# Value blocks and gates of the second projection computed as rows past stationary tokens

## Chip, cores and metric

One core of a Trainium2 chip runs the whole computation in one launch. The metric is device microseconds from start to end. Three runs of the kernel before took 848.38, 850.11 and 849.87 us (median 849.87).

## The reference, cut to what matters

256 tokens of width 1024 pass two transformer blocks in float32. The second block begins with a norm and one wide projection, and the change is in that projection and in what reads it:

```python
proj = h @ w_in[l]                      # 1024 -> qa 512, ka 128, va 128, qb 512, kc 128, vc 128,
                                        #   ksl 128, vsl 128, kw 128, vw 128, gates 24, g_a 1024, g_b 1024
y_a = swa_sink_attention(heads(qa, 8), heads(ka, 2), heads(va, 2), sinks, table_a)
k_cmp = compress(heads(kc, 2), ...); v_cmp = compress(heads(vc, 2), ...)
nsa_gates = jax.nn.sigmoid(g_nsa)       # the 24 gate columns: 8 heads x 3 branches
y_b = nsa_attention(heads(qb, 8), k_cmp, v_cmp, heads(ksl, 2), heads(vsl, 2),
                    heads(kw, 2), heads(vw, 2), nsa_gates, table_b)
merged = jax.nn.sigmoid(g_a) * (y_a @ w_up_a[l]) + jax.nn.sigmoid(g_b) * (y_b @ w_up_b[l])
```

y_b is the gated sum of three attentions: over compressed blocks, over selected blocks (keys ksl, values vsl) and over a window (kw, vw). With 256 tokens the selection takes every block, so both of the latter are plain causal attention.

## The kernel before

**Units.** Every weight matrix is read in units of 1 MB (128 partitions x 2048 numbers), one after the other: SyncE's queue loads a unit into one of three slots of `raw` (`unit`, L357), ScalarE rounds it to `w_hi` (`hi`, L469 and, in loops, L476), VectorE writes the remainder `w_lo` (`lo`, L983; GpSimd helps at some stage borders), TensorE multiplies. The activations are split in the same way into `xh` and `xl`, and each product is three passes: high x high, high x low, low x high. Counting semaphores carry the order: `raw_in`, `hi_done`, `lo_done`, `unit_done`. A load of unit u waits until the low part of unit u - 3 is made.

**The second projection** is 20 units (numbers m below, U_IN2 + m in the code). A unit has 256 columns of weights. The weights stand in the array and the 256 tokens are moved past them, so that results come out with the columns on partitions and tokens along the row (`col_tile`: two halves of 24 products of 256 columns through `passes`, L1719). Units 0 to 2 have a wide form: high part against `xh` and `xl` in one product of 512 columns (`split_high`, L1750), then the low passes (`split_low`, L1758). m = 0 is key and value of the first attention (M_KA), 1 and 2 its queries, 3 the blocks to be compressed, 4 and 5 the queries of y_b, 6 key and value of the selection (M_KS), 7 those of the window (M_KW), 8, 10, 12, 14 and 16 to 19 the wide gates g_a and g_b, 9, 11, 13, 15 the compressing weights (CW). `proj_2` on VectorE drains each unit from PSUM and multiplies by the token's root (`rstd_b`); the semaphore `proj2` counts these drains. For units 0, 6 and 7 it is two operations, key (L1310) and value (L1311).

**The 24 gate columns** do not fit a unit. They are loaded early by themselves (`wg_raw`), split at the start of the stage (ScalarE L645, VectorE L1475), multiplied behind the wide part of unit 1 (24 products, out 24 x 256), scaled by VectorE (L1479), put through a tanh by ScalarE (L693), transposed by TensorE (L2284) and finished by VectorE (L1486). Behind the gate products stands the `spread` (L1911), which brings the roots to all partitions and for which VectorE's copy L1051 waits.

**Values** are needed with tokens on partitions, so TensorE transposes them (`turn_values`, L2215): those of unit 0 in the middle of unit 3, those of units 6 and 7 in the middle of unit 8. ScalarE copies them out (`key_halves`, L676).

**Keys** are needed twice, on either half of the partitions. GpSimd does that in `key_direct`: wait for the drain (`proj2` at 1, 7 and 8 for K_A, K_S and K_W), two DMAs of 64 KB across partitions (L928), two copies (L929, L931). The DMAs of all three count in `key_in`.

**The attention is woven into the units.** `position_time` gives 24 positions, two for each unit from 4 to 7 and from the second half of 9 on; `slot_time`, `turn_time` and `value_time` place 18 slots (three branches of six) on them. A slot is scores on TensorE (L2172), logits and maximum on VectorE (L1341, L1347, L1350), exponentials on ScalarE (L665), transposes (L2187), a copy by ScalarE (L653), and values on TensorE (L2206). Slots 4 and 5, the last of branch 0, have their values at the opening of unit 7's second half; the first scores of branch 1 (slots 6 and 7, keys K_S) open the second half of unit 9 and wait for `key_in[1]`, `kz_direct` at 4 and `kz_ready` at 3. Each engine runs its program in order: on VectorE the attention's work of a position, then the low part of a later unit (`lo` of unit m + 2 in the second half of unit m; that of unit 7 in the first half of unit 6). L1405 is VectorE's strided gather of the blocks, L1510 a residual scaling, L1516 the low part of the blocks. L1178 is the sum of the wide form's two parts.

## Time and profile before

| | before |
|---|---|
| median of three runs | 849.87 us (848.38 to 850.11) |
| profiled execution, its time | 849.17 us |
| its span | 847.4 us |
| TensorE clock granted, mean | 0.997 |
| busy: TensorE / weight loads / VectorE / ScalarE / GpSimd | 835.9 / 736.0 / 646.1 / 442.3 / 88.4 us |
| chain that ended last, by engine | PE 95%, DVE 3%, issue 1%, DMA 1% |
| median time to landing of a 1 MB unit of this projection's matrix | 6.9 us |

The page is one execution. PE is TensorE, DVE VectorE, ACT ScalarE, POOL GpSimd, SP SyncE. A busy matmul is not a matmul at its peak, since matmuls overlap: the step from one start to the next is what one costs. The stage that changes, units 0 to 9 of the second projection, lies between 470 and 540 us.

### The profile page before, as it was taken

To read this page: it belongs to the slowest core of one execution; us is meant where nothing else is said; L and a number is where in the kernel's file an instruction comes from. 1 tells how busy PE (TensorE), PEld (TensorE's weight loads), DVE (VectorE), ACT (ScalarE), POOL (GpSimd) and SP (SyncE) were. 2 spreads that over 40 slices of the span, in tenths; PEclk is the share of its full clock that TensorE was granted. 3 is DMA by queue.
4 is the path that set the end of the run, shared out by engine and by line. 5 is a ranking of instruction groups with operands and counts; after the bars stand their busy time and mean duration, and the time that the engine had idled before them with its cause. 6 is when DMAs were issued, how large, how long until landed. Compare 5 with 4: busy or idle time off the path is not lost.

```text
span 847.4 us, 13897 instructions
## 1 busy us (share of the span) xinstructions
PE 835.9 (99%) x5375; PEld 736.0 (87%) x5375; DVE 646.1 (76%) x816; ACT 442.3 (52%) x562; POOL 88.4 (10%) x70
## 2 busy tenths in 40 slices
PE   9999999999999999999999999999999999999996
PEld 6888888888988888888888899999998988888895
DVE  5786766667967587677676769899775798998997
ACT  6545444546324554544454646476435655665663
POOL 1100000004450300000000400420003000000002
PEclk9999999999999999999999999999999999999998
DMA  8866556554753467665646574657446455466441
GB/s 253 316 231 214 165 197 204 175 198 159 239 167 131 150 224 258 213 214 202 203 153 193 128 191 130 179 164 201 153 149 197 147 199 198 149 203 223 168 174 50
DMA packets 118210, 158.10 MB, mean 187 GB/s; under 512 B 4573, under 2 KB 102285, under 8 KB 118045
## 3 DMA queue, kind: packets, MB, share of 16 engines
q1 hardware_dynamic: 115436, 150.93, 55.4%
q0 software_dynamic: 1488, 5.34, 1.8%
q10 hardware_dynamic: 1248, 1.32, 0.5%
q8 instruction: 26, 0.43, 0.2%
q14 instruction: 12, 0.09, 0.0%
HBM read 154.79 MB, written 1.07 MB: 184 GB/s over the span
## 4 chain that ended last, share of the span: by engine, by line
PE 95%; DVE 3%; issue 1%; DMA 1%; ACT 0%; ACTq 0%; DVEq 0%
PE wk L1750 30%; PE acc L1872 19%; PE wk L1758 16%; PE wk L1719 15%; PE acc L1849 6%; PE acc L1766 1%; PE acc L1719 1%; PE wk L2206 1%; PE acc L2172 1%; DVE w_lo L983 1%; DVE mx L1347 1%; DVE arena L1341 1%; PE acc L1885 1%; DMA x<-in_x 1%; PE wk L2261 0%
## 5 line engine op out<-in xcount | busy, mean ns | idle before, releaser
L1750 PE MATMUL wk<-xhl,w_hi 128*128 128x512 f32 x1104 | 268.8, 391 | 0.0
L1000 DVE TENSOR_TENSOR w_lo<-raw,w_hi 128x2048 fp32r<-128x2048 f32 x83 | 189.9, 2288 | 64.0 <-ACT w_hi L476 62.8
L1750 PEld LDWEIGHTS wk<-xhl,w_hi 128*128 128x128 f32 x1104 | 202.5, 188 | 39.1 <-issue 0.5
L476 ACT ACTIVATE w_hi<-raw 128x2048 fp32r<-128x2048 f32 x83 | 158.0, 1903 | 0.0
L1758 PEld LDWEIGHTS wk<-xhl,w_lo 128*128 128x128 f32 x1104 | 145.4, 191 | 7.9
L1758 PE MATMUL wk<-xhl,w_lo 128*128 128x256 f32 x1104 | 148.1, 283 | 0.0
L983 DVE TENSOR_TENSOR w_lo<-raw,w_hi 128x2048 fp32r<-128x2048 f32 x49 | 113.3, 2314 | 22.7 <-ACT w_hi L469 22.5
L469 ACT ACTIVATE w_hi<-raw 128x2048 fp32r<-128x2048 f32 x53 | 100.8, 1910 | 46.7 <-PE wk L1719 30.2
L1872 PE MATMUL acc<-w_hi,hhl 128*128 128x512 f32 x480 | 119.4, 391 | 0.0
L1719 PE MATMUL wk<-xhl,w_hi 128*128 128x256 f32 x640 | 114.7, 286 | 0.3 <-DVE arena L1323 0.3
L1872 PEld LDWEIGHTS acc<-w_hi,hhl 128*128 128x128 f32 x480 | 88.2, 188 | 17.1
L1719 PEld LDWEIGHTS wk<-xhl,w_hi 128*128 128x128 f32 x640 | 97.4, 191 | 1.7 <-issue 0.8
L1719 PE MATMUL wk<-xhl,w_lo 128*128 128x256 f32 x320 | 85.5, 283 | 0.0
L1872 PE MATMUL acc<-w_lo,hhl 128*128 128x512 f32 x240 | 59.3, 389 | 0.0
L1719 PEld LDWEIGHTS wk<-xhl,w_lo 128*128 128x128 f32 x320 | 59.1, 191 | 0.0
L1872 PEld LDWEIGHTS acc<-w_lo,hhl 128*128 128x128 f32 x240 | 45.1, 188 | 9.3
L842 POOL TENSOR_TENSOR w_lo<-raw,w_hi 128x1024 fp32r<-128x1024 f32 x4 | 9.6, 2390 | 349.6 <-DVE w_lo L990 349.6
L539 ACT ACTIVATE hhl<-work 128x512 fp32r<-128x512 f32 x20 | 12.7, 633 | 56.4 <-PE acc L1872 45.9
L524 ACT ACTIVATE work<-wk 128x512 f32<-128x512 f32 x22 | 13.1, 598 | 54.9 <-PE wk L1758 54.8
L762 ACT ACTIVATE work<-work,conv 128x256 f32<-128x256 f32 x44 | 24.1, 595 | 33.3 <-DVE work L1577 30.1
L1586 DVE SCALAR_TENSOR_TENSOR work<-work,conv 128x255 f32<-128x255 f32 (+1 forms) x88 | 37.5, 478 | 1.8 <-ACT work L762 1.8
L533 ACT ACTIVATE work<-work 128x512 f32<-128x512 f32 x22 | 13.9, 632 | 40.2 <-DVE work L1076 40.2
(277 smaller groups left out, 964.8 us busy)
## 6 DMA issues: line engine op xcount, KB each, us to landing
raw<-in_ffn_w SPq DMA_DIRECT2D x65, 1024.0 KB, 5.2
raw<-in_w_in SPq DMA_DIRECT2D x26, 1024.0 KB, 6.9
raw<-in_w_ffn_in SPq DMA_DIRECT2D x22, 1024.0 KB, 5.0
raw<-in_w_ffn_out SPq DMA_DIRECT2D x11, 1024.0 KB, 4.8
raw<-in_w_out SPq DMA_DIRECT2D x8, 1024.0 KB, 4.8
arena<-bias_scratch POOLq DMA_DIRECT2D x4, 512.0 KB, 6.3
raw<-in_cmp_w_k SPq DMA_DIRECT2D x2, 1024.0 KB, 5.5
raw<-in_cmp_w_v SPq DMA_DIRECT2D x2, 1024.0 KB, 6.5
```

The lines of the kernel that those rows point to most:

```text
L469: nc.scalar.activation(w_hi[:, u % SLOTS], raw[:, u % SLOTS], ACT.Copy).then_inc(hi_done, 1)
L476: nc.scalar.activation(w_hi[:, s], raw[:, s], ACT.Copy).then_inc(hi_done, 1)
L533: nc.scalar.activation(t_s, a_s, ACT.Tanh, scale=0.5).then_inc(tanh_out, 1)
L762: nc.scalar.activation(k_n(dst, 2)[:, t], k_n(src, 2)[:, t], ACT.Identity, scale=conv[:, 2, bass.ds(f, 1)], bias=conv[:, 3, bass.ds(f, 1)]) \
L983: nc.vector.tensor_tensor(w_lo[:, s], raw[:, s], w_hi[:, s].bitcast(F32), ALU.subtract) \
L1000: nc.vector.tensor_tensor(w_lo[:, s], raw[:, s], w_hi[:, s].bitcast(F32), ALU.subtract) \
L1586: nc.vector.scalar_tensor_tensor(out=new, in0=tile[:, 0:T - back], scalar=conv[:, 2 - back, bass.ds(f, 1)], in1=new, op0=ALU.mult, op1=ALU ...
L1719: mm = nc.tensor.matmul(dst, w, v, start=start and n == 0, stop=stop and n == len(pairs) - 1, skip_group_check=True)
L1750: mm = nc.tensor.matmul(bank, wh[:, c, cols], xhl[:, c].rearrange("p n t -> p (n t)"), start=c == 0, stop=False, skip_group_check=True)
L1758: mm = nc.tensor.matmul(bank[:, 0:T], wl[:, c, cols], xh[:, c], start=False, stop=c == DC - 1, skip_group_check=True)
L1849: mm = nc.tensor.matmul(acc[:, b], w, v[:, c, cols], start=opens and c == 0 and n == 0, stop=end and n == 2, skip_group_check=True)
L1872: mm = nc.tensor.matmul(acc[:, b], hhl[:, c, side, rows], w[:, c, cols], start=opens and n == 0 and c == 0, stop=False, skip_group_check=True)
```

## The change

The column blocks are dealt out anew. Unit 6 becomes `M_ROWS`: the value blocks of selection and window (128 columns each) and the 24 gate columns, 280 columns in all, and it is multiplied the other way round: the tokens stand in the array (two tiles of 128) and the 280 columns of weights are moved past them (`value_rows`, 48 products of 280 columns). Results come out with tokens on partitions, into PSUM banks 0 and 3 of `wk`. Unit 7 becomes `M_KEYS`, the two key blocks, in the old form.

Both units are loaded by two DMAs of 128 columns each (`unit_pair`). The high and low parts of unit 6 are written with a pitch of 280, beside those of the gate columns, which are split at the same point (`hi_rows`, `lo_rows`) and no longer at the start of the stage. The gate products, their scaling, the two gate transposes, the four value transposes in unit 8 and their two copies by ScalarE go. The spread stands behind unit 1's low passes. The drain of unit 6 is four operations with the root as a scalar for each partition (24 and 256 columns for each token tile), that of unit 7 one of 512 columns. TensorE waits for the drain of unit 6 before the values of slot 4, which write bank 3. The gates' tanh comes in unit 8, their affine step in unit 9. GpSimd waits for the eighth drain instead of the seventh before it carries K_S.

```diff
-IN2_COLS = (512, 0, 256, 1280, 768, 1024, 1536, 1792, 2072, None, 2328, None, 2584, None, 2840, None,
+IN2_COLS = (512, 0, 256, 1280, 768, 1024, None, None, 2072, None, 2328, None, 2584, None, 2840, None,
             3096, 3352, 3608, 3864)
-M_KA, M_QA, M_CMP, M_QB, M_KS, M_KW = 0, (1, 2), 3, (4, 5), 6, 7
+M_KA, M_QA, M_CMP, M_QB, M_ROWS, M_KEYS = 0, (1, 2), 3, (4, 5), 6, 7
+NG = 24
+RW = UC + NG
...
-        w_hi = sb("w_hi", [P, SLOTS, UNIT], F32R)
-        w_lo = sb("w_lo", [P, SLOTS, UNIT], F32R)
+        w_hi_all = sb("w_hi", [P, SLOTS * UNIT + DC * NG], F32R)
+        w_lo_all = sb("w_lo", [P, SLOTS * UNIT + DC * NG], F32R)
+        w_hi, w_lo = (t[:, 0:SLOTS * UNIT].rearrange("p (s n) -> p s n", s=SLOTS) for t in (w_hi_all, w_lo_all))
+        rows_hi, rows_lo = (t[:, (SLOTS - 1) * UNIT:].rearrange("p (k n) -> p k n", k=DC) for t in (w_hi_all, w_lo_all))
...
-        v2 = [carve(60 + n, 2, P) for n in range(2)]
+        v_sw = carve(60, 2, 2, P)
+        v2 = [carve(20, 2, P), v_sw[:, 0], v_sw[:, 1]]
...
+            def unit_pair(u, src, col, first):
+
+                sp.wait_ge(lo_done, u - 2)
+                dst = k_n(raw[:, u % SLOTS], DC)
+                sp.dma_start(dst[:, :, 0:P], src[:, :, col:col + P]).then_inc(first, 16)
+                sp.dma_start(dst[:, :, P:UC], src[:, :, col + UC:col + UC + P]).then_inc(raw_in[u % SLOTS], 16)
...
+                elif m in (M_ROWS, M_KEYS):
+                    unit_pair(U_IN2 + m, w2, 1664 if m == M_ROWS else 1536, pair_in[m - M_ROWS])
+                    continue
...
-            act.wait_ge(wg_in, 16)
-            nc.scalar.activation(wg_hi[:], wg_raw, ACT.Copy).then_inc(wg_split, 1)
...
-            def key_halves(n):
-
-                act.wait_ge(value_turned, n + 1)
-                if n == 2:
-                    act.wait_ge(pv_mm, 6)
-                bank = acc[:, (0, 0, 1)[n]]
-                nc.scalar.activation(v2[n % 2], k_n(bank[:, T:2 * T], 2), ACT.Copy).then_inc(kz_ready, 1)
+            def values_copy():
+
+                act.wait_ge(value_turned, 1)
+                nc.scalar.activation(v2[0], k_n(acc[:, 0, T:2 * T], 2), ACT.Copy).then_inc(kz_ready, 1)
+
+            def hi_rows(u):
+
+                act.wait_ge(wg_in, 16)
+                act.wait_ge(unit_done, u - 2)
+                nc.scalar.activation(rows_hi[:, :, UC:], wg_raw, ACT.Copy)
+                act.wait_ge(pair_in[0], 16)
+                act.wait_ge(raw_in[u % SLOTS], raw_count(u))
+                nc.scalar.activation(rows_hi[:, :, 0:UC], k_n(raw[:, u % SLOTS], DC), ACT.Copy).then_inc(hi_done, 1)
...
-                if m == 2:
-                    act.wait_ge(gate_scaled, 1)
-                    nc.scalar.activation(g_f, g_f, ACT.Tanh, scale=0.5).then_inc(gate_tanhed, 1)
...
-                        hi(U_IN2 + m + 2)
+                        if m + 2 == M_ROWS:
+                            hi_rows(U_IN2 + m + 2)
+                        else:
+                            if m + 2 == M_KEYS:
+                                act.wait_ge(pair_in[1], 16)
+                            hi(U_IN2 + m + 2)
...
-                        key_halves(1)
-                        key_halves(2)
+                        act.wait_ge(proj2, M_ROWS + 1)
+                        nc.scalar.activation(gates[:], gates[:], ACT.Tanh, scale=0.5).then_inc(gate_tanhed, 1)
...
-            key_direct(1, 7)
+            key_direct(1, 8)
             key_direct(2, 8)
-            pool.wait_ge(value_turned, 3)
+            pool.wait_ge(value_turned, 1)
...
-                if m in (M_KA, M_KS, M_KW):
-                    n = {M_KA: K_A, M_KS: K_S, M_KW: K_W}[m]
-                    nc.vector.tensor_tensor(kf[:, n], src[:, 0], rstd_b[:], ALU.mult)
-                    nc.vector.tensor_tensor(v_f[n % 2], src[:, 1], rstd_b[:], ALU.mult).then_inc(proj2, 1)
+                if m == M_KA:
+                    nc.vector.tensor_tensor(kf[:, K_A], src[:, 0], rstd_b[:], ALU.mult)
+                    nc.vector.tensor_tensor(v_f, src[:, 1], rstd_b[:], ALU.mult).then_inc(proj2, 1)
                     return
-                if m == M_CMP:
+                if m == M_ROWS:
+                    for tt in range(2):
+                        rows, root = wk[:, 3 * tt, 0:RW], both_r[:, 2 + tt:3 + tt]
+                        nc.vector.tensor_scalar(gates[:, tt], rows[:, UC:], root, None, ALU.mult)
+                        done = nc.vector.tensor_scalar(v_sw[:, :, tt], k_n(rows[:, 0:UC], 2), root, None, ALU.mult)
+                    done.then_inc(proj2, 1)
+                    return
+                if m == M_KEYS:
+                    dst = kf[:, K_S:K_W + 1]
...
+            def lo_rows(u):
+
+                dve.wait_ge(hi_done, u + 1)
+                nc.vector.tensor_tensor(rows_lo[:, :, UC:], wg_raw, rows_hi[:, :, UC:].bitcast(F32), ALU.subtract)
+                nc.vector.tensor_tensor(rows_lo[:, :, 0:UC], k_n(raw[:, u % SLOTS], DC),
+                                        rows_hi[:, :, 0:UC].bitcast(F32), ALU.subtract).then_inc(lo_done, 1)
...
-                    dve.wait_ge(wg_split, 1)
-                    nc.vector.tensor_tensor(wg_lo[:], wg_raw, wg_hi[:].bitcast(F32), ALU.subtract) \
-                        .then_inc(wg_split, 1)
                     rstd_both()
-                    dve.wait_ge(gate_mm, 1)
-                    nc.vector.tensor_tensor(g_f, acc[0:24, 0, 0:T], rstd_b[0:24], ALU.mult).then_inc(gate_scaled, 1)
                 elif m - 1 not in CW and m not in CW:
                     proj_2(m - 1)
-                if m == 3:
-
-                    dve.wait_ge(gate_turned, 1)
-                    turned = acc[:, 0, 0:64].rearrange("p (t n) -> p t n", t=2)[:, :, 0:24]
-                    nc.vector.tensor_scalar(gates[:], turned, 0.5, 0.5, ALU.mult, ALU.add).then_inc(gate_taken, 1)
+                if m == 9:
+                    dve.wait_ge(gate_tanhed, 1)
+                    nc.vector.tensor_scalar(gates[:], gates[:], 0.5, 0.5, ALU.mult, ALU.add).then_inc(gate_taken, 1)
...
+                    if half and m + 2 == M_ROWS:
+                        lo_rows(U_IN2 + m + 2)
+                    elif half and m and m != 5:
...
-                            pe.wait_ge(kz_ready, 3 if r else 1)
+                            if r == 0:
+                                pe.wait_ge(kz_ready, 1)
...
+                        if s == 4:
+                            pe.wait_ge(proj2, M_ROWS + 1)
...
+            def value_rows(tt, dst):
+
+                rows = slice(tt * P, (tt + 1) * P)
+                for c in range(DC):
+                    mm = passes(dst, ((xh[:, c, rows], rows_hi[:, c]), (xh[:, c, rows], rows_lo[:, c]),
+                                      (xl[:, c, rows], rows_hi[:, c])), c == 0, c == DC - 1)
+                return mm
...
+                    elif m == M_ROWS:
+                        mm = value_rows(half, wk[:, 3 * half, 0:RW])
...
-                    if at == (1, 0):
-                        pe.wait_ge(wg_split, 2)
-                        for c in range(DC):
-                            mm = passes(acc[0:24, 0, 0:T], ((wg_hi[:, c], xh[:, c]), (wg_hi[:, c], xl[:, c]),
-                                                            (wg_lo[:, c], xh[:, c])), c == 0, c == DC - 1)
-                        mm.then_inc(gate_mm, 1)
+                    if at == (1, 1):
                         spread(3, acc[:, 1])
-                    if at == (2, 0):
-                        pe.wait_ge(gate_tanhed, 1)
-                        for tt in range(2):
-                            mm = nc.tensor.transpose(acc[:, 0, tt * 32:tt * 32 + 24], g_f[:, tt * P:(tt + 1) * P],
-                                                     ident[0:24, 0:24])
-                        mm.then_inc(gate_turned, 1)
                     if at == (3, 0):
                         pe.wait_ge(proj2, 1)
-                        pe.wait_ge(gate_taken, 1)
-                        turn_values(K_A, acc[:, 0])
-                    if at == (8, 0):
-                        pe.wait_ge(proj2, 8)
-                        pe.wait_ge(logit_out, 6)
-                        for n in (K_S, K_W):
-                            turn_values(n, acc[:, n - 1])
```

## Rows read from the trace of the kernel before

**Rows 1.** The page's part 1: busy time, share of the span, instructions.

```profile
PE 835.9 (99%) x5375; PEld 736.0 (87%) x5375; DVE 646.1 (76%) x816; ACT 442.3 (52%) x562; POOL 88.4 (10%) x70
```

**Rows 2.** Stretch table: window, length, busy PE, PEld, DVE, ACT, POOL, clock, DMA.

```profile
498.00:522.00 24.00, 22.99 (x246) 21.82 (x246) 19.83 (x37) 14.06 (x37) 1.04 (x2) 1.00 0.35 98
```

**Rows 3.** TensorE's timeline at unit 7's start: start, us, operation, [idle before, releaser].

```profile
521.72 0.69 PE L2206 MATMUL wk<-arena 128*64 128x64 f32 x16 [1.01 <-DVE w_lo L983]
```

**Rows 4.** TensorE's timeline, units 1 and 2: wide, gates, spread, wide, low.

```profile
476.90 3.82 PE L1750 MATMUL wk<-xhl,w_hi 128*128 128x512 f32 x16
...
480.56 0.40 PE L1719 MATMUL acc<-xhl,wg_hi 128*24 128x256 f32 x2
...
483.33 0.38 PE L1911 MATMUL acc<-cst,both_r 128*128 128x128 f32 x2
...
485.45 3.82 PE L1750 MATMUL wk<-xhl,w_hi 128*128 128x512 f32 x16
...
489.43 2.18 PE L1758 MATMUL wk<-xhl,w_lo 128*128 128x256 f32 x16
```

**Rows 5.** TensorE's timeline in unit 8, around the value transposes.

```profile
533.08 0.40 PE L1719 MATMUL wk<-xhl,w_hi 128*128 128x256 f32 x2
...
533.44 0.60 PE L2215 MATMUL acc<-cst,sq 128*128 128x128 f32 x4
...
534.11 0.28 PE L1719 MATMUL wk<-xhl,w_lo 128*128 128x256 f32 x1
```

**Rows 6.** TensorE's timeline: values of slots 4 and 5, scores of slot 6.

```profile
526.50 1.15 PE L2206 MATMUL wk<-arena 128*64 128x64 f32 x32
...
537.99 0.70 PE L2172 MATMUL acc<-arena 64*128 64x256 f32 x4
```

**Rows 7.** Timeline of ScalarE and VectorE at the start of the stage.

```profile
477.24 0.37 ACT L645 ACTIVATE wg_hi<-work 128x192 fp32r<-128x192 f32 x1
...
477.64 0.36 DVE L1475 TENSOR_TENSOR wg_lo<-work,wg_hi 128x192 fp32r<-128x192 f32 x1 [0.42 <-ACT wg_hi L645]
477.91 0.15 DVE L1040 SCALAR_TENSOR_TENSOR nr<-sums_x 128x2 f32<-128x2 f32 x1
...
483.75 0.42 DVE L1051 COPY rstd_b<-acc 128x256 f32<-128x256 f32 x1 [0.59 <-PE acc L1911]
```

**Rows 8.** VectorE's timeline: first logits, strided gather, drains of units 6, 7.

```profile
498.79 0.69 DVE L1341 SCALAR_TENSOR_TENSOR arena<-acc,arena 128x512 f32<-128x512 f32 x1 [0.48 <-PE acc L2172]
...
512.84 0.57 DVE L1405 TENSOR_TENSOR arena<-sq,vec 64x240 f32<-64x240 f32 x1
...
526.15 0.42 DVE L1310 TENSOR_TENSOR sq<-wk,rstd_b 128x256 f32<-128x256 f32 x1
526.48 0.42 DVE L1311 TENSOR_TENSOR sq<-wk,rstd_b 128x256 f32<-128x256 f32 x1
...
531.55 0.42 DVE L1310 TENSOR_TENSOR sq<-wk,rstd_b 128x256 f32<-128x256 f32 x1
```

**Rows 9.** Landing times: second key DMA of K_A, K_S, K_W; loads issued 487.5 to 496.5.

```profile
arena<-sq POOLq DMA_DIRECT2D x1, 64.0 KB, 5.0
...
arena<-sq POOLq DMA_DIRECT2D x1, 64.0 KB, 6.1
...
arena<-sq POOLq DMA_DIRECT2D x1, 64.0 KB, 6.6
...
DMA to landing us min/median/max: 7.9/7.9/8.3
```

**Rows 10.** GpSimd's timeline: the key DMAs of K_A, K_S, K_W, first copy behind K_W's.

```profile
485.58 1.13 POOL L928 DMA_DIRECT2D arena<-sq  x2 [11.63 <-DVE sq L1311]
...
527.19 1.03 POOL L928 DMA_DIRECT2D arena<-sq  x2 [27.29 <-DVE sq L1311]
...
533.21 1.03 POOL L928 DMA_DIRECT2D arena<-sq  x2 [4.08 <-issue]
534.28 1.61 POOL L929 COPY arena<-sq 64x256 f32<-64x256 f32 x1
```

More of the change, by code:

```diff
@@ L234, in build @@
         hv_rep = sqf[:, 2 * T:3 * T].rearrange("p (n m) -> p n m", n=2)
-        v_f = [sqf[:, n:n + T] for n in (1280, 1536)]
-        g_f = sqf[0:24, 1792:2048]
+        v_f = sqf[:, 1280:1536]
         prob_c = sqf[:, 1280:1536].rearrange("p (m c) -> p m c", c=16)
@@ L242, in build @@
         wg_raw = work[:, 5, T:T + 192].rearrange("p (k n) -> p k n", k=DC)
-        wg_hi, wg_lo = sb("wg_hi", [P, DC, 24], F32R), sb("wg_lo", [P, DC, 24], F32R)
         conv = sb("conv", [P, 4, 44])
@@ L306, in build @@
             sem(n) for n in ("bias_mm", "bias_cmp_mm", "bias_row", "bias_written", "bias_ready"))
-        wg_split, gate_mm, gate_scaled, gate_tanhed, gate_turned, gate_taken = (
-            sem(n) for n in ("wg_split", "gate_mm", "gate_scaled", "gate_tanhed", "gate_turned",
-                             "gate_taken"))
+        gate_tanhed, gate_taken = (sem(n) for n in ("gate_tanhed", "gate_taken"))
+        pair_in = [sem(f"pair_in{n}") for n in range(2)]
         proj2, value_turned, kz_zero, kz_direct, kz_ready = (
@@ L708, in _ @@
                             act.wait_ge(hi_done, U_IN2 + m + 2)
-                        hi(U_IN2 + m + 2)
+                        if m + 2 == M_ROWS:
[4 more added lines that the diff above has]
+                            hi(U_IN2 + m + 2)
                     if (m, half) == (3, 1):
-                        key_halves(0)
+                        values_copy()
                     if (m, half) == (7, 1):
@@ L1307, in proj_2 @@
                 both = bcast(rstd_b[:], 2)
-                if m in (M_KA, M_KS, M_KW):
-                    n = {M_KA: K_A, M_KS: K_S, M_KW: K_W}[m]
-                    nc.vector.tensor_tensor(kf[:, n], src[:, 0], rstd_b[:], ALU.mult)
-                    nc.vector.tensor_tensor(v_f[n % 2], src[:, 1], rstd_b[:], ALU.mult).then_inc(proj2, 1)
+                if m == M_KA:
+                    nc.vector.tensor_tensor(kf[:, K_A], src[:, 0], rstd_b[:], ALU.mult)
+                    nc.vector.tensor_tensor(v_f, src[:, 1], rstd_b[:], ALU.mult).then_inc(proj2, 1)
                     return
-                if m == M_CMP:
+                if m == M_ROWS:
[7 more added lines that the diff above has]
+                    dst = kf[:, K_S:K_W + 1]
+                elif m == M_CMP:
                     dst = kf[:, K_CK:K_CV + 1]
@@ L1503, in _ @@
                         proj_2(m - 1)
-                    if half and m and m != 5:
+                    if half and m + 2 == M_ROWS:
+                        lo_rows(U_IN2 + m + 2)
+                    elif half and m and m != 5:
                         lo(U_IN2 + m + 2)
@@ L2207, in attend_values, with turn_values @@
                                                           prob_t[:, t0 // HD, s % 2, n],
-                                                          v2[r % 2][:, kc, g * HD:(g + 1) * HD], start=kc == 0,
+                                                          v2[r][:, kc, g * HD:(g + 1) * HD], start=kc == 0,
                                                           stop=kc == b)
                         mm.then_inc(pv_mm, 1)
-            def turn_values(n, bank):
+            def turn_values():
                 for tt in range(2):
-                    mm = nc.tensor.transpose(bank[:, T + tt * P:T + (tt + 1) * P], v_f[n % 2][:, tt * P:(tt + 1) * P],
-                                             ident)
+                    mm = nc.tensor.transpose(acc[:, 0, T + tt * P:T + (tt + 1) * P], v_f[:, tt * P:(tt + 1) * P], ident)
                 mm.then_inc(value_turned, 1)
+            def value_rows(tt, dst):
[4 more added lines that the diff above has]
+                return mm
             def turn_y(n):
@@ L2273, in _ @@
                     at = (m, half)
[L2274 to L2286 removed]
+                    if at == (1, 1):
+                        spread(3, acc[:, 1])
                     if at == (3, 0):
                         pe.wait_ge(proj2, 1)
[L2289 to L2295 removed]
+                        turn_values()
                     if at == (16, 0):
```

## The prediction

> **What bounds the kernel now.** I read the page's first part, then the idle stretches and waits of TensorE in the stage that changes, then that stage's timeline engine by engine. The page gives TensorE 835.9 us of a span of 847.4 us [rows 1]: whatever TensorE no longer has to do should come off the end, unless somebody makes it wait instead. In the stage from 498 to 522 us it is busy 22.99 of 24.00 us [rows 2]. The missing 1.01 us is one wait, at the start of unit 7, for VectorE's low part L983 [rows 3]. So TensorE is the bound in this stage, but VectorE's chain is right behind it, and in one place ahead of it. Two more arrivals decide this case: when unit 7's second half opens at 526.50 (values of slots 4 and 5), and when the first scores of branch 1 open at 537.99 [rows 6], since those read the selection keys K_S that GpSimd has carried to the other partitions by DMA.
>
> **What TensorE gets back.** (a) The 24 gate products (8 chunks, three each) start at 480.56 and the spread behind them at 483.33: 2.77 us [rows 4]. (b) The two gate transposes: 16 wide products take (480.56 - 476.90) = 3.66 us where the next work follows at once, 0.229 us each; those from 485.45 would let the next start at 489.11, it starts at 489.43 [rows 4]: 0.32 us. (c) The four transposes of K_S and K_W values, 533.44, with the next product pair effectively at 534.11 - 0.24 = 533.87: 0.43 us [rows 5]. **What it pays:** 48 products of 280 columns instead of 256. Products of 256 come every (533.44 - 533.08) / 3 = 0.120 us, of 512 every 0.229 [rows 4, 5], so by the line between them 24 columns cost 0.010 us, 48 of them 0.48 us. No row has 280 columns; the bounds are nothing and the price of 512 columns, 48 x 0.109 = 5.2 us. I take the line, as 280 is next to 256. Sum on TensorE alone: 2.77 + 0.32 + 0.43 - 0.48 = 3.0 us.
>
> **The early stage follows.** The spread moves behind unit 1's 16 low passes, which take 16 x 0.12 = 1.9 us, and so comes at 480.56 + 1.9 = 482.5 instead of 483.33. The roots it needs come from twelve small steps of VectorE that begin at 477.91 and take about 0.2 us each, so they end near 480.2 and, without the gate subtraction, earlier. VectorE's copy follows the spread by 0.42 us [rows 4, 7], then two halves of the first drain, the low part of unit 3 and the sum for unit 1: from 482.9 some 0.42 + 0.7 + 2.2 + 0.7 = 4.0 us, done near 486.9; TensorE wants unit 3 behind 16 wide and 16 low passes, at 482.6 + 3.7 + 1.9 = 488.2. Cover stays, 1.3 us; if it were gone, each us late would come off the gain. So at unit 3's end everything is 2.77 + 0.32 = 3.09 us earlier. There VectorE waits for TensorE (0.48 us before the first logits at 498.79 [rows 8]), so its chain starts 3.09 us earlier too.
>
> **VectorE's chain gets longer.** From 498.79 on stand, one behind the other, logits on VectorE, their exponentials and then unit 6's high part on ScalarE, its low part on VectorE, and VectorE's work without a gap up to unit 7's low part, for which TensorE waits at 521.72 [rows 3, 8]. Into this chain go the gate subtraction on VectorE, 0.27 us from its start to the next one's (477.64 to 477.91, of 0.36 us busy), and the 192-element gate copy on ScalarE, 0.37 us busy and with the same overlap 0.27 us [rows 7]; together 0.54 us. They cost nothing where they stood and their full price here. The big copies now write with a row pitch of 280; the nearest strided row is L1405, 0.57 us for 240 elements [rows 8]. Its runs are single elements, these are 256 long, so I take no extra; the bound is below, as a rival. The load of unit 6 is two DMAs with runs of 512 bytes: it is issued near 486.2 and needed when ScalarE comes to it, after 500, where three loads of 1 KB runs take 7.9 to 8.3 us to land [rows 9]; it may take half as long again. Unit 7 starts 3.09 - 0.54 = 2.55 us earlier, and TensorE's own 0.48 us there is inside its wait of 1.01 us.
>
> **Two new waits.** At the second half of unit 7 TensorE, due at 526.50 - 2.55 = 523.95, must wait for the rows drain (proj2 at 7). VectorE starts it at 526.15 - 2.55 = 523.60 [rows 8]. It was two operations 0.33 us apart; it is now two of 256 (0.33 each) and two of 24 columns, between 0.1 and 0.15 each (0.15 us busy for 2 columns [rows 7]): about 0.92 us, done 524.5. TensorE waits 0.6 us, with the values, their drain and the half unit queued behind it. With (c) its way to the scores of branch 1 is then 2.55 - 0.6 + 0.43 = 2.4 us shorter: arrival 535.6. The gates' tanh (ScalarE) and affine step (VectorE) move to units 8 and 9, behind no queue that TensorE waits for; nearly 0.6 us of transfers of turned values leave ScalarE there.
>
> The second wait is the keys. Before, K_S left unit 6: GpSimd started its two DMAs at 527.19, and TensorE wanted them at 537.99, 4 us after they had landed. Now K_S and K_W both come from unit 7, and GpSimd's wait is for the eighth drain. VectorE reaches that drain at 531.55 - 2.45 (the rows drain takes back 0.1 or more) = 529.1 and ends it, as one operation of 512 columns at 0.69 us [rows 8], at 529.8. What follows has three cases here. The second DMA is issued about 0.52 us after the first (two in 1.03 us) and lands 5.0, 6.1 and 6.6 us after its issue. K_A: 485.58 + 0.57 + 5.0 = 491.15, from a drain that ended 0.3 us before the issue: 5.9 us. K_S: drain ended 526.48 + 0.42 = 526.9, landed 527.19 + 0.52 + 6.1 = 533.8: 6.9 us. K_W: drain ended 531.55 + 0.33 + 0.42 = 532.3, issued only at 533.21, landed 533.73 + 6.6 = 540.3: 8.0 us [rows 8 to 10]. I take K_W's, because the new K_S stands in exactly its place: behind the drain of unit 7, with the same three long VectorE operations following (L1516, L983, L1510), beside which GpSimd's first copy took 1.61 us [rows 10], and between the same two 1 MB loads. That gives 529.8 + 8.0 = 537.8 us, against 537.99 before. **Behind the scores nothing is removed**, so the whole change is worth what is left at this point: 0.2 us.
>
> The Trainium skill, page "DMA: Bandwidth & Descriptors", section "Anatomy of one DMA", gives a DMA from GpSimd about 2.0 us plus its bytes at 436 GB/s, and "SBUF — State Buffer", section "Who interferes with whom", says that a VectorE tensor_tensor with two SBUF inputs blocks GpSimd's reads but not its descriptor writes. By these K_S would land near 533 (an estimate), which is the rival of keys in time, below. This trace agrees on the stretched copy [rows 10] and not on the 2 us: the three landings took 5.0 to 6.6 us from issue [rows 9].
>
> **The rivals.** *Keys in time* (K_A's 5.9 us: 529.8 + 5.9 = 535.7, or sooner): TensorE's path alone counts, 2.4 us, 847.5. For it: K_A's row under just as many loads. Against: K_W's row. *Keys like the old K_S*, 6.9 us: scores at 536.7, 1.3 us gained, 848.6. For it: it is the same pair of copies. Against: VectorE was on PSUM operands behind it, and is not now. *Slower, the strided split*: if the high and low parts of unit 6, written at a pitch of 280, cost what L1405 pays per element (0.57 / 240 = 2.4 ns, 2048 elements, 4.9 us against 0.69 / 512 x 2048 = 2.8 us at most), VectorE's chain grows by 2.1 us or more and the keys with it, since they have no cover: 1.9 to 2.4 us slower, near 852. It decides as soon as the two parts together cost more than 0.2 us extra. *It doesn't do what it says*: 280 columns priced like 512, TensorE 4.7 us later than reckoned, of which 1.06 us vanish in the wait at unit 7 and 0.6 us in that for the rows drain: 3.0 us behind 535.6, 538.6, so 0.6 us slower, 850.5.
>
> **How the numbers follow.** The profiled execution took 849.17 us (span 847.4); the median of three is 849.87, and I forecast against the median: 849.87 - 0.2 = 849.7. About 0.2% (1.7 us) is what a measurement can tell from no change. Chances: forecast 0.48; keys like K_S 0.22 (within 0.2% as well); keys in time 0.20, faster; 280 columns 0.02, also within 0.2%; strided split 0.05, slower; 0.03 for keys over 1.9 us later than K_W's row, slower. So faster 0.20, same 0.72, slower 0.08. The range goes down to keys in time, 847.4, and up to 850.6, a landing 0.9 us later than K_W's (it and K_S's are 1.1 us apart).
>
> **What would show it.** First wide product of unit 2 and so on 3.1 us earlier by unit 3's end; TensorE idle about 1.1 us at unit 7 for VectorE's low part, 0.6 us at its second half for the rows drain; 48 products 0.130 us apart; and about 2 us idle before the scores of branch 1, ended by GpSimd's DMA. The prediction is wrong if that last wait is missing or short (then faster), or if unit 6's copies take visibly longer than their like do (then slower).

## The result, and the profile after

22 runs of each kernel: before 848.54 us (median; 848.28 to 850.11), after 850.12 us (848.38 to 851.46). Ratio after to before 1.0012, 95% interval 1.0007 to 1.0018: about 1.0 us slower, where 0.2 us faster was forecast (the medians alone lie 1.6 us apart, the means 1.15: each kernel's times fall into two groups, and the median stands in the larger). The 22 times of the changed kernel form two groups, seven from 848.4 to 849.2 and fifteen from 850.0 to 851.5. Of those of before 17 lie below 848.9 and five from 849.5 up.

| | before | after |
|---|---|---|
| median of 22 runs | 848.54 us | 850.12 us |
| profiled execution, its time / its span | 849.17 / 847.4 us | 850.15 / 848.3 us |
| TensorE clock granted, mean | 0.997 | 0.996 |
| busy: TensorE / VectorE / ScalarE / GpSimd | 835.9 / 646.1 / 442.3 / 88.4 us | 833.1 / 646.2 / 441.6 / 88.9 us |

The page of after, part 1 (against [rows 1]):

```profile
PE 833.1 (98%) x5343; PEld 733.4 (86%) x5345; DVE 646.2 (76%) x816; ACT 441.6 (52%) x560; POOL 88.9 (10%) x70
```

TensorE has 2.8 us less to do and the span is 0.9 us longer. So it waits more. The waits of TensorE from 440 to 620 us of after (total, times, longest):

```profile
PE acc L2200 <- DMA arena<-sq: 2.4, 1, 2.4
PE wk L2236 <- DVE arena L1333: 0.9, 1, 0.9
PE wk L2236 <- DVE w_lo L1000: 0.7, 1, 0.7
PE wk L1746 <- DVE arena L1348: 0.3, 1, 0.3
```

The first is the wait for the keys. Around it, TensorE's timeline of after (start, us, operation, [idle before, releaser]):

```profile
534.87 0.28 PE L2300 MATMUL wk<-w_hi,mhl 128*64 128x256 f32 x1
537.55 2.08 PE L2200 MATMUL acc<-arena 64*128 64x256 f32 x8 [2.41 <-DMA arena<-sq]
539.56 0.42 PE L2298 MATMUL wk<-w_lo,mhl 128*32 128x256 f32 x1
539.78 0.41 PE L2300 MATMUL wk<-w_hi,mhl 128*64 128x256 f32 x1
...
540.63 0.28 PE L2300 MATMUL wk<-w_hi,mhl 128*64 128x256 f32 x1
540.75 0.28 PE L2298 MATMUL wk<-w_lo,mhl 128*32 128x256 f32 x1
```

The eight scores take 2.01 us to the next product, the products behind them follow each other by 0.21 us, and from 540.63 on by 0.12. That is one kind of work at two speeds. The stretches of that time in after tell why (length, busy TensorE, granted clock, busy share of the DMA engines, GB/s):

```profile
537.40:539.40 2.00, 1.84 (x8) 0.50 0.82 259
539.40:541.00 1.60, 1.60 (x11) 0.62 0.13 47
```

The granted clock stood at 0.50, the lower of its two levels (1.2 GHz), from 537.2 to 540.6 us: it fell behind 2.1 us without work, 0.3 us ahead of the end of the wait. In before, the same stretches have

```profile
537.40:539.40 2.00, 2.00 (x17) 1.00 0.99 269
```

**One clock for all traces.** Everything ahead of this stage is the same code in both kernels, and yet the traces reach it at different times: unit 1's wide products start at 476.90 in before [rows 4] and at 476.14 in after.

```profile
476.14 3.82 PE L1777 MATMUL wk<-xhl,w_hi 128*128 128x512 f32 x16
```

What is gained or lost ahead of that point is not the change's: e3_keys_first and e10_keys_first_again below are one kernel and reach it at 477.15 and 476.13, and all twelve traces of this document lie between 476.13 and 477.58. So I measure all runs from it. In after the scores of branch 1 start at 537.55 - 476.14 = 61.41 us, in before at 537.99 - 476.90 = 61.09. The next product starts at 63.42 against 62.16, and the span ends at 372.16 against 370.50. The change so costs this execution 1.66 us: 0.32 us because the scores start later, 0.94 us because they take longer, 0.4 us behind them.

### The profile page after: what moved, and what is told of

Its sections match the earlier page's. It is cut to its first block, busy times and chain, and to the rows that moved or that the text cites. A ratio compares the mean times of both kernels' runs of the same rounds, so it can differ in the third digit from the quotient of the medians.

```text
span 848.3 us, 13832 instructions
## 1 busy us (share of the span) xinstructions
PE 833.1 (98%) x5343; PEld 733.4 (86%) x5345; DVE 646.2 (76%) x816; ACT 441.6 (52%) x560; POOL 88.9 (10%) x70
## 3 DMA queue, kind: packets, MB, share of 16 engines
HBM read 154.79 MB, written 1.07 MB: 184 GB/s over the span
## 4 chain that ended last, share of the span: by engine, by line
PE 92%; DVE 5%; DMA 2%; issue 0%; ACT 0%; ACTq 0%; POOL 0%; DVEq 0%
PE wk L1777 30%; PE acc L1899 19%; PE wk L1785 16%; PE wk L1746 14%; PE acc L1876 6%; DVE w_lo L1000 1%; PE acc L1793 1%; DMA arena<-sq 1%; PE acc L2200 1%; DMA x<-in_x 1%; PE acc L1746 1%; DVE mx L1372 1%; DVE arena L1366 1%; PE acc L1912 1%; PE wk L2236 1%
## 5 line engine op out<-in xcount | busy, mean ns | idle before, releaser
L1777 PEld LDWEIGHTS wk<-xhl,w_hi 128*128 128x128 f32 x1104 | 202.5, 188 | 38.9 <-issue 0.2
L1785 PEld LDWEIGHTS wk<-xhl,w_lo 128*128 128x128 f32 x1104 | 145.5, 191 | 8.0
L1785 PE MATMUL wk<-xhl,w_lo 128*128 128x256 f32 x1104 | 147.9, 282 | 0.0
L1746 PE MATMUL wk<-xhl,w_hi 128*128 128x256 f32 x608 | 108.7, 286 | 0.3 <-DVE arena L1348 0.3
L1746 PEld LDWEIGHTS wk<-xhl,w_hi 128*128 128x128 f32 x608 | 92.5, 191 | 1.6 <-issue 0.8
L1746 PE MATMUL wk<-xhl,w_lo 128*128 128x256 f32 x304 | 81.0, 283 | 0.0
L1746 PEld LDWEIGHTS wk<-xhl,w_lo 128*128 128x128 f32 x304 | 56.0, 191 | 0.0
L674 ACT ACTIVATE arena<-arena,nmx 128x256 f32<-128x256 f32 (+1 forms) x48 | 21.4, 446 | 26.9 <-DVE nmx L1375 26.6
```

What stands on the lines that cost most here:

```text
L674: ex = nc.scalar.activation(prob[s % 2][:, cols], logit[s % 2][:, cols], ACT.Exp, bias=nmx[:, r, b, h0 + h:h0 + h + 1], accum_out=sums[:, ...
L1746: mm = nc.tensor.matmul(dst, w, v, start=start and n == 0, stop=stop and n == len(pairs) - 1, skip_group_check=True)
L1777: mm = nc.tensor.matmul(bank, wh[:, c, cols], xhl[:, c].rearrange("p n t -> p (n t)"), start=c == 0, stop=False, skip_group_check=True)
L1785: mm = nc.tensor.matmul(bank[:, 0:T], wl[:, c, cols], xh[:, c], start=False, stop=c == DC - 1, skip_group_check=True)
```

## The experiments

Each was timed against the kernel before, but for e8_after_again, which is a single execution. e5_few_gates leaves out six of the eight chunks of the gate sums; all others compute the whole. The table has for each profiled execution the times from unit 1's wide products on, and the median of all runs:

| run | scores of branch 1 | next product | end | half clock behind the scores | median | ratio to before, 95% interval |
|---|---|---|---|---|---|---|
| before | 61.09 | 62.16 | 370.50 | no | 848.5 to 848.8 | |
| after | 61.41 | 63.42 | 372.16 | yes | 850.12 | 1.0012 (1.0007 to 1.0018) |
| e8_after_again | 61.93 | 63.00 | 371.36 | no | 849.25, one run | |
| e1_warm | 61.20 | 62.26 | 370.59 | no | 848.76 | 1.0002 (0.9993 to 1.0011) |
| e7_warm5 | 61.22 | 62.28 | 370.62 | no | 849.89 | 1.0005 (0.9996 to 1.0014) |
| e2_act_keys | 61.13 | 62.77 | 372.14 | yes | 848.93 | 1.0004 (0.9995 to 1.0014) |
| e4_late_keys | 63.67 | 65.51 | 374.64 | yes | 852.87 | 1.0040 (1.0026 to 1.0054) |
| e6_load_behind | 58.93 | 60.00 | 369.23 | no | 847.33 | 0.9982 (0.9973 to 0.9991) |
| e5_few_gates | 59.01 | 60.08 | 368.43 | no | 846.54 | 0.9975 (0.9966 to 0.9984) |
| e3_keys_first | 58.22 | 59.28 | 368.25 | no | 846.40 | 0.9975 (0.9966 to 0.9985) |
| e10_keys_first_again | 58.19 | 59.25 | 368.17 | no | 846.49 | 0.9978 (0.9967 to 0.9988) |
| e9_late_wait | 56.88 | 57.94 | 368.03 | no | 846.29 | 0.9970 (0.9958 to 0.9981) |

### Is it the clock? Dummy products in the wait

```diff
+                            if r == 1:
+                                pe.wait_ge(y_taken, 2)
+                                keep_warm(10)
                             pe.wait_ge(key_in[r], 16 * 2)
```

> The kernel after, with ten dummy products of 512 columns (zeros, 2.1 us at full clock) in TensorE's program right before its wait for the keys of branch 1; nothing else changes. Theory A (the wait lets the clock fall to half for 3.4 us, and that is what makes the change slower instead of equal): the granted clock stays at 1.00 through units 9 and 10, the eight score products take about 1.1 us instead of 2.08, and the kernel ends 1.4 us sooner than the kernel after, ratio to the kernel before 1.000 (848.5 to 848.8 us). The wait for the DMA itself stays, shortened to about 0.3 us behind the dummies. Rival B (the late keys alone are the loss, the clock dip costs nothing that the end sees): time as after, ratio 1.001 to 1.002.

TensorE's timeline of e1_warm at the scores:

```profile
535.21 2.33 PE L1808 MATMUL wk<-zeros 128*128 128x512 bf16 x10
537.51 1.13 PE L2203 MATMUL acc<-arena 64*128 64x256 f32 x8
538.57 0.31 PE L2301 MATMUL wk<-w_lo,mhl 128*32 128x256 f32 x1
```

`keep_warm` writes to a bank of `wk`, hence the wait for `y_taken`. The ten dummies fill the wait, the scores start where they did (61.20 for 61.41) and take 1.06 us to the next product in place of 2.01. The end comes at 370.59, within 0.1 us of before. So filling the wait with useless work gives back 1.57 us of this execution's loss of 1.66. Of that, 1.34 us is the lower clock and 0.21 us an earlier start of the scores. Of the eleven executions of e1_warm none took more than 849.62 us, where fifteen of the 22 of after took 850.0 or more.

### The changed kernel once more

> The changed kernel once more, one look; nothing is left out. Its times lie near 848.5 and near 850.5. If the clock's fall decides between the two, a profiled execution near 848.5 shows the same wait of 2.4 us ahead of the scores and no half clock behind it, and one near 850 shows the half clock.

The same kernel, TensorE's timeline at the scores, and the stretch behind them:

```profile
538.07 1.13 PE L2200 MATMUL acc<-arena 64*128 64x256 f32 x8 [2.39 <-DMA arena<-sq]
539.14 0.30 PE L2298 MATMUL wk<-w_lo,mhl 128*32 128x256 f32 x1
```

```profile
539.40:541.00 1.60, 1.60 (x16) 1.00 0.36 111
```

The same wait (2.39 us for 2.41), and no fall of the clock: the scores take 1.07 us and from there to the end it is 308.36 us, as in before (308.34), where after has 308.74. So two executions of one kernel with one wait differ by 0.94 + 0.38 = 1.3 us through the clock alone. This one has lost 0.5 us elsewhere, in a wait of 0.7 us for ScalarE ahead of the scores that the first does not have.

Are the two groups of times of after the executions with and without the fall? The others have no trace, but each has its mean granted clock. The three traces of this document with the fall (after, e2_act_keys, e4_late_keys) have 0.996, e8_after_again has 0.998. Of the fifteen slower executions of after thirteen have 0.996 and two 0.994; of the seven faster ones five have 0.997 or 0.998 and two 0.996. That agrees, but for the last two. It is no proof for a single execution, since every trace also holds a stretch at half clock at the very end of the program (in before from 842.1 us on), of varying length: e3_keys_first has 0.996 without a fall at the scores.

The second, smaller group of before is of another kind. Of the executions of before beside e1_warm the three from 849.67 to 850.00 us have 0.997, and the others have 0.996 to 0.998. An arrival at unit 1 that is 1 us later, as between e3_keys_first and e10_keys_first_again, would make such a group; that is not shown for these executions.

### A wait of half the length

The edit of e1_warm with `keep_warm(5)`.

> The changed kernel with 5 dummy products of 512 columns (in place of 10) ahead of the wait for the K_S keys; nothing is left out. TensorE then idles about 1.2 us ahead of the scores in place of 2.4 (none with 10). If an idle of that length is too short to bring the clock down, the time is that of the run with 10 products, 848.7, with no half clock in the record. If any idle of a microsecond brings it down, 850.1 with the half clock for some 3.4 us.

```profile
536.42 1.25 PE L1808 MATMUL wk<-zeros 128*128 128x512 bf16 x5
538.80 1.13 PE L2203 MATMUL acc<-arena 64*128 64x256 f32 x8 [1.12 <-DMA arena<-sq]
```

In this execution an idle stretch of 1.12 us behind dummies brought no fall, and from unit 1 to the end it equals e1_warm (370.62, 370.59). It reached unit 1 late, at 477.58, and its 849.97 us comes from there. The median of 849.89 lies 1.1 us above that of e1_warm, since six of the eleven executions took 849.9 to 850.2 us, and by the times alone both expectations stay open. The granted clocks speak against a fall: all six have 0.997, like the traced one among them, and of the eleven a single one, of 849.20 us, has the 0.996 of the traces with a fall. So the late group looks like late arrivals; one trace shows it, for the other executions it is not shown.

### The same wait in the kernel before

```diff
-            key_direct(1, 7)
+            key_direct(1, 8)
```

> The kernel before with one number changed: GpSimd waits for the eighth drain instead of the seventh before it carries K_S. All products, splits and transposes stay. Theory A (that wait with its clock dip is a full cost): K_S is issued near 533.2 and lands near 540.3, TensorE waits 2.3 us from 537.99, the clock falls as in the kernel after and costs 1.4 us more: 3.7 us slower, ratio 1.004. Rival B (VectorE's work behind the scores has slack of 1.5 us and takes up part of it, and a wait of this length does not move the clock): under 2 us, ratio 1.002 or less.

```profile
540.13 1.90 PE L2172 MATMUL acc<-arena 64*128 64x256 f32 x8 [2.53 <-issue]
541.97 0.42 PE L2261 MATMUL wk<-w_lo,mhl 128*32 128x256 f32 x1
```

The landing in this kernel is late by the same step: GpSimd waits for the eighth drain. The end moves by 374.64 - 370.50 = 4.14 us: 2.58 us for the scores' start, 0.77 us for their length and 0.79 us behind, the last two with the clock at half. Here the fall costs 1.56 us. The order of the keys alone makes both the wait and the fall, with nothing else of the change in the kernel.

Its five executions also part the two costs. Three took 852.87 to 853.08 us, with a mean clock of 0.996 or 0.994; two took 851.08 and 851.13, with 0.998. The two lie 2.5 us above before's 848.64, which is the later start of the scores and nothing more; the three lie another 1.8 us above them.

### Is an early microsecond worth one at the end?

```diff
-                        for c in range(DC):
+                        for c in (0, DC - 1):
                             mm = passes(acc[0:24, 0, 0:T], ((wg_hi
```

> The kernel before with the 24 gate products cut to 6 (chunks 0 and 7 alone; six of the eight chunks of the gate sums are left out, so the gates are not the reference's). It takes 18 products of 0.1155 us, 2.08 us, off TensorE at the stage's start and changes nothing later. Theory A (time saved early on TensorE arrives at the end unless a later wait takes it; in before the K_S keys landed in time, with little to spare): 846.5, ratio 0.9975, and the wait at the scores of branch 1 stays small, since the keys of before leave one unit earlier and move forward with TensorE. Rival B (the stage is bound by something else, so that early TensorE time is worth nothing): 848.6, ratio 1.000.

The scores start at 59.01 for 61.09, 2.08 us earlier, which is 18 x 0.1155 us to the last digit, and the end comes 2.07 us earlier. TensorE is the bound of the stage, and in before the keys leave early enough to follow. That part of the forecast's reasoning holds, in a kernel whose gates are wrong.

### Who holds the keys up? First try: the issuing engine

GpSimd no longer sends the K_S keys (its loop leaves them out); ScalarE does, behind the high part of unit 10:

```diff
+                        act.wait_ge(proj2, M_KEYS + 1)
+                        for g in range(2):
+                            dst, src = slice(HD * (1 - g), HD * (2 - g)), slice(HD * g, HD * (g + 1))
+                            act.dma_start(kz[1][dst, g], kf[src, 1]).then_inc(key_in[1], 16)
```

> The kernel after, with the two DMAs of K_S alone issued from ScalarE's queue, behind the high part of unit 10 and on the same eighth drain, instead of from GpSimd; GpSimd keeps its two copies and the other keys. Theory A (what counts is only when K_S lands, and it lands late because GpSimd's DMAs start late beside VectorE's work): issue near 530.2, landing 3 to 4.5 us later, near 533.7 to 535, so TensorE, due at 535.1, hardly waits, the clock does not fall, and the 2.4 us of its own path reach the end: ratio 0.997 to 0.998. Rival B (the landing is long because of the 1 MB loads in flight, whoever issues): landing near 536.5, TensorE waits over 1 us, ratio 0.999 to 1.001.

```profile
530.25 2.15 ACTq L736 DMA_DIRECT2D arena<-sq  x2
...
538.39 1.71 PE L2204 MATMUL acc<-arena 64*128 64x256 f32 x8 [2.10 <-DMA arena<-sq]
```

The landings took 7.0 us from issue here and 6.9 in after. The scores start at 61.13 for 61.41 and still wait 2.10 us. The theory that GpSimd's queue makes the keys late has fallen. Its median is low (848.93), yet the profiled execution took 851.17: the clock fell in it, and it reached unit 1 at 477.26, 1.1 us later than after. Five of its eleven executions have a mean clock of 0.998, so the fall seems rarer here; why, no trace shows.

### Second try: the load that shares the engines

SyncE issues the 1 MB load of unit 12 behind the keys' landing:

```diff
+                if m == 12:
+                    sp.wait_ge(key_in[1], 16 * 2)
                 unit(U_IN2 + m, src, DC)
```

> The changed kernel, but SyncE issues the 1 MB load of unit 12 only when both halves of the K_S keys have landed, so that the keys do not share the DMA engines with it; nothing is left out. Theory B (the keys land late since they share the engines with that load: 6.9 us from issue against 4.4 where the keys left earlier): they land 2 us or more sooner, about 535.3 for 537.5, TensorE's wait at the scores of branch 1 falls to 0.5 or less, the clock does not fall, and the time is 850.1 - 1.4 (clock) - 2.0 (wait) = 846.7, ratio 0.998, as long as unit 12's own load is in time (its rounding on ScalarE started 7 us after its landing). Theory C (the landing of two 64 KB key blocks takes 6 to 7 us by itself): wait and time as in the changed kernel, 2.4 us and 850.1, or more if unit 12 then comes late.

In after the load goes out just ahead of the keys:

```profile
528.50 0.37 SPq L359 DMA_DIRECT2D raw<-in_w_in  x1
...
529.37 1.03 POOL L945 DMA_DIRECT2D arena<-sq  x2 [33.40 <-DVE sq L1348]
```

Issue and landing of the two K_S blocks: first after, then e6_load_behind (DMAs issued from 529.2 to 531 and from 529 to 531; the last number is the median time from issue to landing).

```profile
arena<-sq POOLq DMA_DIRECT2D x2, 64.0 KB, 6.9
```

```profile
arena<-sq POOLq DMA_DIRECT2D x2, 64.0 KB, 1.9
```

The timeline of e6_load_behind, GpSimd and the load's queue, and TensorE at the scores:

```profile
529.49 1.03 POOL L947 DMA_DIRECT2D arena<-sq  x2 [33.40 <-DVE sq L1350]
...
531.93 0.37 SPq L359 DMA_DIRECT2D raw<-in_w_in  x1
...
535.20 1.13 PE L2202 MATMUL acc<-arena 64*128 64x256 f32 x8
```

That is the cause of the late keys. In after the load was issued at 528.50, 0.87 us ahead of the keys, and they took 6.9 us. With the load behind them they took 1.9 us, and TensorE goes into the scores with no wait. One line turns the change into a gain of 1.4 us (0.8 to 2.3 by the interval). The gain at the scores was 61.09 - 58.93 = 2.16 us; 0.9 us is lost behind them (309.23 us from the next product to the end, 308.34 in before). Set beside before product by product, TensorE loses 0.3 us of its lead in the 16 transposes at 541.15 (0.97 us for 0.66) and 0.5 us around a wait of 0.26 us for VectorE's drain, at 550.17. e3_keys_first below loses the same 0.5 us at the same wait (550.02) without holding any load, so that part is not the price of the held load.

Here the Trainium skill, page "DMA: Bandwidth & Descriptors", section "Anatomy of one DMA", is near after all: the 2.0 us plus bytes that the prediction set aside (2.15 us for 64 KB, an estimate from that page) is about what the block takes with the load held back (1.9 us). The same page, section "Queues, rings and completion order", says that each engine takes turns between the queues that have work for it, which fits a small block slowed by a large one; no run here shows the turns themselves.

### Keys first

The two units change places: keys as unit 6, value rows as unit 7. K_S then leaves one unit earlier, as in before. The extra 24 columns of the weight slot move to its front, the rows use one bank of each of `wk` and `acc`, and TensorE's waits follow.

```diff
-M_KA, M_QA, M_CMP, M_QB, M_ROWS, M_KEYS = 0, (1, 2), 3, (4, 5), 6, 7
+M_KA, M_QA, M_CMP, M_QB, M_KEYS, M_ROWS = 0, (1, 2), 3, (4, 5), 6, 7
...
-            key_direct(1, 8)
-            key_direct(2, 8)
+            key_direct(1, 7)
+            key_direct(2, 7)
...
-                        if s == 4:
-                            pe.wait_ge(proj2, M_ROWS + 1)
```

> The kernel after with its two new units exchanged: unit 6 holds the keys, unit 7 the 280 columns (drained from banks wk 1 and acc 1), so GpSimd carries K_S behind the seventh drain as before; the gate columns are split with unit 7, and the wait for the rows drain before slot 4 is gone. Theory A (the form of the unit is good, only its place is bad): 3.1 us early, 0.27 us given back in VectorE's chain before unit 7, 0.48 us for 280 columns now uncovered, 0.43 us from the value transposes: 2.8 us, ratio 0.9967, with TensorE never waiting for keys and the clock at 1.00. Rival B (VectorE's chain or the larger drain at unit 8 takes the gain whatever the order): ratio 0.999 or more, with TensorE waiting for VectorE in units 7 to 9.

> The kernel of e3_keys_first once more, beside the run before it; nothing is left out. 846.4, ratio 0.9975, no half clock in the record before the end of the program; its runs show which of the two is the faster on one chip.

TensorE's timeline of e3_keys_first: its one long wait, the rows' products, the scores.

```profile
519.06 1.15 PE L2234 MATMUL wk<-arena 128*64 128x64 f32 x32 [1.28 <-DVE w_lo L1438]
...
521.15 0.42 PE L1744 MATMUL wk<-w_hi,xhl 128*128 128x280 f32 x2
521.41 0.29 PE L1744 MATMUL wk<-w_lo,xhl 128*128 128x280 f32 x1
521.53 0.42 PE L1744 MATMUL wk<-w_hi,xhl 128*128 128x280 f32 x2
...
535.37 1.14 PE L2200 MATMUL acc<-arena 64*128 64x256 f32 x8
```

846.4 and 846.5 us: faster than both kernels, on two chips. The wait for the keys is gone, and so is the one for the rows' drain; the scores start 2.87 us earlier than in before, of which 0.6 us is lost behind them. All that the change takes off TensorE arrives at the scores once the keys are in time, and 2.25 us of it at the end. The products of 280 columns are 0.129 us apart (21 of them from 521.15 to 523.86), against the 0.130 of the forecast.

### The last wait of that version

TensorE waits for VectorE's low part of the rows only behind the 32 value products and 16 turns that don't read it.

```diff
-                if not 0 < m < WIDE_IN2:
+                if not 0 < m < WIDE_IN2 and m != M_ROWS:
                     pe.wait_ge(lo_done, u + 1)
...
                         attend(k)
+                    if (m, half) == (M_ROWS, 0):
+                        pe.wait_ge(lo_done, u + 1)
```

> The kernel of e3_keys_first (keys as unit 6, value rows as unit 7) with TensorE's wait for the low part of the value rows put behind the 32 value products and 16 turns that stand between the two units, which do not need it; nothing is left out. Of that run's wait of 1.28 us at VectorE's low part (TensorE resumes at 519.06, needs the part 1.72 us later) nothing should be left: 846.4 - 1.3 = 845.1, ratio 0.996. Rival (the wait only moves: the turns behind the values then wait for ScalarE's exponentials, or VectorE, which is busy to 523.4, holds the later steps): 846.4, ratio 0.9975, with a new wait in the trace between 517 and 530.

```profile
517.44 1.15 PE L2234 MATMUL wk<-arena 128*64 128x64 f32 x32
...
533.75 1.13 PE L2200 MATMUL acc<-arena 64*128 64x256 f32 x8
...
536.87 0.48 PE L1744 MATMUL wk<-xhl,w_hi 128*128 128x256 f32 x2 [0.94 <-DVE arena L1348]
```

The wait of 1.28 us is gone, and the scores start 1.3 us earlier (56.88 for 58.19 and 58.22). Behind them stands a new wait of 0.94 us for VectorE's drain of unit 8. That drain starts at 536.03 - 476.87 = 59.16 us here and at 59.27 us in e3_keys_first: VectorE hardly noticed that TensorE was earlier. In both runs one of its operations ahead of the drain is stretched by 1.6 us while GpSimd casts 2048 columns for 1.9 us: the residual scaling L1535 here (2.92 us for 1.28), the gates' affine step L1511 in e3_keys_first (1.76 us for 0.19). The cast waits for TensorE and so moves with it; no run without the cast was made. The rival holds, in a place that its text did not name. 0.1 to 0.2 us is left in the profiled executions, and the medians (846.29, 846.49 beside it) don't tell the two apart.

## Why the prediction was wrong, step by step

Times of after with 0.76 us added, so that they stand on the clock of before.

- **TensorE's savings: right.** 2.77 us of gate products, 0.32 and 0.43 us of transposes, 0.48 us for the wider products: the sum said 3.0 us, the page says 835.9 - 833.1 = 2.8 us busy (some records can be missing). At unit 3's end the forecast was 3.09 us earlier. VectorE's first logits started at 498.79 in before [rows 8] and at 495.62 here, 3.17 us earlier:

```profile
494.86 0.69 DVE L1366 SCALAR_TENSOR_TENSOR arena<-acc,arena 128x512 f32<-128x512 f32 x1 [0.48 <-PE acc L2200]
```

- **VectorE's longer chain, and no price for the strided split: right.** The two parts of the rows on VectorE:

```profile
501.60 0.36 DVE L1437 TENSOR_TENSOR w_lo<-work,w_hi 128x192 fp32r<-128x192 f32 x1 [3.22 <-ACT w_hi L691]
501.88 2.28 DVE L1438 TENSOR_TENSOR w_lo<-raw,w_hi 128x2048 fp32r<-128x2048 f32 x1
```

  The gate part takes 0.28 us to the next start (0.27 forecast), the rows' 2.28 us, what a low part without a pitch takes. The rival of the strided split fell, and so did that of 280 columns priced like 512.

- **Two waits of TensorE: right in kind.** For the low part of unit 7 0.7 us (1.1 forecast), for the rows' drain 0.85 us (0.6 forecast). The drain's four operations start 0.15, 0.39 and 0.15 us apart: the narrow ones as reckoned, the wide ones 0.39 where 0.33 was taken, so the drain ends 1.16 us behind its start (0.92 forecast):

```profile
522.71 0.23 DVE L1332 TENSOR_SCALAR gates<-wk,both_r 128x24 f32<-128x24 f32 x1
522.86 0.47 DVE L1333 TENSOR_SCALAR arena<-wk,both_r 128x256 f32<-128x256 f32 x1
523.25 0.23 DVE L1332 TENSOR_SCALAR gates<-wk,both_r 128x24 f32<-128x24 f32 x1
523.40 0.47 DVE L1333 TENSOR_SCALAR arena<-wk,both_r 128x256 f32<-128x256 f32 x1
...
528.39 0.68 DVE L1348 TENSOR_TENSOR sq<-wk,rstd_b 128x512 f32<-128x512 f32 x1
```

  TensorE reached the scores at 537.55 - 2.41 = 535.14, so 535.9 (535.6 forecast).

- **The keys: right in kind, 0.5 us too optimistic.** Their drain starts at 529.15 (529.1 forecast). They landed by 538.31, 8.5 us behind its end, where the row of K_W gave 8.0. So the scores started 0.32 us later than in before, not 0.2 us earlier. The forecast took the landing as a property of the block's place and chose its row well, but had no cause for it. The cause is the load of unit 12 (6.9 us beside it, 1.9 without), and with it named the one-line remedy would have been in sight.

- **"Behind the scores nothing is removed, so the whole change is worth what is left at this point": the step that failed.** Nothing is removed there, but something is added. The forecast had the wait ("about 2 us idle before the scores", 2.41 measured) and treated it as time that only passes. TensorE's clock fell behind it: 0.94 us in the scores and 0.4 us behind them in after, 1.6 us in the other two executions where it fell. With this term at nothing the 0.2 us of gain stood alone; with the 0.5 us of the keys it is a loss of 0.3, and with 1.3 us of clock on top, in most executions but not in all, it is about what was measured. The rivals moved the keys' landing or a cost in the chain; none had a price that starts with the wait itself. The signs that the prediction set itself did not catch it either: the wait was there and of the length forecast, and no sign looked at what stands behind it.

That the measured median lies only 0.4 us from the forecast 849.7 is luck. The forecast started from a median of three, 849.87, and more runs put before at 848.54; the error of the start and that of the change cancel in part.

## What to carry to other kernels

When an edit turns busy time of TensorE into a wait of two microseconds, count the lower clock behind the wait as well as the wait. Where TensorE is the bound, as here, weigh whether a few dummy products in the wait are cheaper. A small transfer that TensorE waits for is priced by the loads that are in flight beside it: issue it ahead of them, or hold the load for it if the load has slack. If two units of work are regrouped, the one whose result has the longest way to its reader (here drain, GpSimd, DMA) goes first.

## What the runs showed of the hardware

- **An idle TensorE of 2.1 to 2.5 us brought the clock down in three executions of four.** It fell behind waits of 2.41 (after), 2.10 (e2_act_keys) and 2.53 us (e4_late_keys), and not behind one of 2.39 us (e8_after_again) or 1.12 us (e7_warm5). Ahead of each wait TensorE was busy and its clock at full. In after the clock fell 0.3 us ahead of the end of the wait, in e2_act_keys and e4_late_keys 0.4 and 0.2 us after TensorE had begun the scores. The fall cost 1.3 to 1.6 us. The Trainium skill, page "TensorE: Matmul & The Clock Gate", section "Wait — 56ns, not 53.3ns?", gives the step from one matmul to the next as its columns over the clock, with 2.5 ns more at the higher level: 213 and 109 ns for 256 columns (an estimate from that page). The trace agrees nearly, with 0.21 us (five steps from 539.56 to 540.63) and 0.12 us (540.63 to 540.75). What decides, with the same wait, whether the clock falls is not settled by these runs.
- **A 64 KB block across partitions takes 1.9 us with the load held back and 6.9 us beside a 1 MB load** issued 0.9 us ahead of it; which engine issues it made no difference (7.0 us from ScalarE's queue).
- **Products of 280 columns cost 0.129 us**, on the line between 256 (0.120) and 512 (0.229).
